# A two-layer decoder trunk: 32 of 80 modulation pieces scaled by ScalarE and added by GpSimd's transfers in place of VectorE

## The chip, the cores and the metric

The kernel runs on one core of a Trainium2 chip, as one launch. The metric is the device time of that launch in microseconds (us). An execution under the profiler gives the trace that is read below; its own time stands beside its span.

## The reference, cut to what matters

Two layers over 256 tokens of 1024 features, all in float32:

```python
mod = silu(c) @ w_ada + b_ada                  # 6 parts of 1024: sh1, sc1, gt1, sh2, sc2, gt2
h = rmsnorm(x, g_pre_mix) * (1 + sc1) + sh1
... = split(h @ w_in)                          # queries, keys, values, index heads, gates
x = x + gt1 * rmsnorm(mixed @ w_out, g_post_mix)
h = rmsnorm(x, g_pre_ffn) * (1 + sc2) + sh2
f = (silu(h @ w_gate) * (h @ w_up)) @ w_down   # 2816 hidden features
x = x + gt2 * rmsnorm(f, g_post_ffn)
```

`mixed` is the gated sum of two attentions. The modulation `mod` depends only on the vector `c`. It is a product of a row of 1024 with a matrix of 1024 x 6144 in each layer, so its work is mostly the reading of 24 MB of weights.

## The kernel before, in words

**Products.** Every matrix product of weights runs on TensorE as three passes: high part times high part, high times low, low times high. ScalarE makes the high part of a weight unit (`split_hi`, L769, a rounding copy of 128 x 2048), VectorE the low part (`split_lo`, L1156, unit minus high part). Units of 1 MB come from one stream in memory through three buffers (`raw`) and go on to a ring of five split units (`w_hi`, `w_lo`). SyncE, called SP here, issues their loads (L579); a load waits until VectorE has split the unit that had the buffer.

**The feed-forward part** works through 11 blocks of 256 hidden features. In block j TensorE makes gate and up products for token tile 0, then for tile 1 (`up`), then the down products of block j-1 for tile 0, turns the gated products of block j for both tiles (`turn_m`, L1853), and makes the down products for tile 1. For each tile ScalarE takes the silu (L906) and VectorE multiplies it with the up product (`gate_m`, L1224). ScalarE and VectorE then split the turned products into high and low parts (`m_hi_split`, L862; `m_lo_split`, L1458). ScalarE's order in a block is: split of the unit `ahead`, silu of tile 0, silu of tile 1, split of the first unit `behind`, high parts of both turned tiles, split of the second unit `behind`.

In layer 1, blocks 5, 6 and 8, 9 go in pairs as a twin (seven products in place of eight). Twins need sums of the input over token tiles and halves (`add_tokens`). These are made in two parts, between the two `gate_m` calls of a block: part 0 (L1195 to L1197) in the block before `sums_step`, part 1 (L1189, L1191) in block `sums_step`. For layer 1 `sums_step` is 2. For layer 0, which has no twins, it is 11, so that part 0 runs in block 10.

**Modulation.** The 10 tables that are not made at the start are each made of 8 pieces of `w_ada` (128 x 1024, 512 KB); pieces are counted from 0 to 79. SP loads a piece (L589) into one of two slots (`ada`, `ADA_RING` = 2), once the piece two before it has been used. VectorE multiplies it with a column of silu(c) and adds it to the table's buffer in one instruction (`add_pieces`, L1284) and so frees the slot. After 8 pieces GpSimd sums over the partitions (`reduce`, L666, two all-reduces), loads the table's gains over the buffer (`finish`, L673, a transfer that GpSimd issues) and VectorE combines the two (`make_table`, L1343); for a shift table GpSimd copies the sum instead (L677). There are three such buffers. Each is first zeroed and given its bias by GpSimd (`seed`, L656 and a transfer of 4 KB, L659).

Pieces 0 to 23 and 48 to 71 are used in the mixing parts, 24 to 47 in layer 0's feed-forward part, 72 to 79 in layer 1's. `ffn_pieces(l)` gives their number for each block, and the blocks in which `make_table` stands. Of three pieces in a block, one is used after the split of the unit `ahead`, one before and one after the second unit `behind`. The order of work on each engine is written out by hand; SP issues weight and piece loads from one queue, in the same order in which they are used. The table that is made last (layer 1's gt2) is needed by the closing norm.

Of the kernel before, what the change touches and what calls it, by code (L numbers as in the profile page):

```python
# [13 lines left out]
KT = D // P  # L14
# [182 lines left out]
def mix_pieces(l, s):  # L197

    return (MIX_PIECES | {1: (1, 0), 2: (2, 1)} if l else FIRST_PIECES).get(s, (0, 0))
TOP_STEPS = range(5, 5 + N_TOP // 16)  # L200


def ffn_pieces(l):

    if l + 1 < DEPTH:
        return (0, 2, 3, 3, 3, 3, 3, 3, 2, 2, 0), (4, 8)
    return (2, 2, 3, 0, 0, 0, 0, 0, 1, 0, 0), (10,)

# [42 lines left out]
def hybrid_decoder_trunk(nc, x_in, c_in, const_in, c_row, scale_first, shift_first, w_ada, b_ada, gains, w_stream, out):  # L251
    with ExitStack() as ctx:
# [147 lines left out]
        s_m = sem("m_ready")  # L400
        s_adause = sem("ada_used")
        s_table = sem("table_made")
        s_dve = sem("dve_chain")
# [57 lines left out]
        def piece_at(n):  # L461

            return ada[:, n % ADA_RING, :], s_ada[n % ADA_RING], 16 * (n // ADA_RING + 1)

        def mm_no(c, t):
# [79 lines left out]
        def sums_step(l):  # L545

            return TWINS[l][0] - 3 if TWINS[l] else N_FF

# [12 lines left out]
        def _(sp):  # L561
# [19 lines left out]
            def load_pieces(count):  # L581
                for _ in range(count):
                    n = pieces[0]
                    l, part = MADE[n // KT]
                    dst, landed, _ = piece_at(n)
                    if n >= ADA_RING:
                        sp.wait_ge(s_adause, n - ADA_RING + 1)
                    k = n % KT
                    sp.dma_start(dst, w_ada[l, k * P:(k + 1) * P, part * D:(part + 1) * D]).then_inc(landed, 16)  # L589
                    pieces[0] += 1  # L590
# [52 lines left out]
        def _(pool):  # L643
# [17 lines left out]
            def reduce(n, i):  # L661

                pool.wait_ge(s_adause, KT * (n + 1))
                for half in range(2):
                    cols = slice(512 * half, 512 * half + 512)
                    nc.gpsimd.partition_all_reduce(acc[:, cols], tables[i][:, cols], P,  # L666
                                                   bass.bass_isa.ReduceOp.add).then_inc(s_reduced, 1)
                    pool.wait_ge(s_reduced, 2 * n + half + 1)

            def finish(n, i, l, which):  # L670
# [47 lines left out]
            for l in range(DEPTH):  # L718
# [18 lines left out]
                if more:  # L737
                    pool.wait_ge(s_h, 8 * l + 4)
                    seed(scale_t, l + 1, SC1, s_bias[1])
                    seed(shift_t, l + 1, SH1, s_bias[2])  # L740
                finish(n + 3, 0, l, 3)
                if more:
                    pool.wait_ge(s_table, 4 * l + 3)
                    finish(n + 4, 1, l + 1, 0)
                    pool.wait_ge(s_table, 4 * l + 4)
                    finish_shift(n + 5, 2 * l + 2)
# [3 lines left out]
        def _(act):  # L750
            def split_hi(l, u, part=None):
# [17 lines left out]
                nc.scalar.activation(w_hi[:, U % RING, a:n], src[:, a:n], ACT.Copy).then_inc(s_hi, 1)  # L769

            def copy_chunk(l, c, t):
# [136 lines left out]
            def twin_hi(l, j):  # L908
# [16 lines left out]
                m_hi_split(l, j, 0)  # L925
                m_hi_split(l, j, 1)
                split_hi(l, behind[6])
                split_hi(l, behind[7])
                m_hi_split(l, j + 1, 0)
                m_hi_split(l, j + 1, 1)  # L930

            def sum_squares(n):
# [100 lines left out]
            for l in range(DEPTH):  # L1033
# [60 lines left out]
                call_root(2 * l)  # L1094
                border(l, True)
                for j, *both in ffn_steps(l):
                    if both:
                        twin_hi(l, j)
                        continue
                    ahead, behind = up_splits(l, j)  # L1100
                    for u in ahead[:1]:
                        split_hi(l, u)
                    if j == 1:
                        m_hi_split(l, 0, 1)
# [13 lines left out]
                    if j < N_FF - 1:  # L1118
                        split_hi(l, behind[0])
                        if j:  # L1120
                            m_hi_split(l, j, 0)
                            m_hi_split(l, j, 1)
                        split_hi(l, behind[1])
                    else:
                        split_hi(l, behind[1])
                        call_root(2 * l + 1)
                        m_hi_split(l, j, 1)
# [4 lines left out]
        def _(dve):  # L1132
# [50 lines left out]

            def add_tokens(l, part):

                upper, lower = slice(0, 4), slice(4, KT)
                one, two = slice(0, P), slice(P, 2 * P)
                if part:
                    link(nc.vector.scalar_tensor_tensor(out=sums[:, upper, one], in0=sums[:, lower, two], scalar=-1.0,  # L1189
                                                        in1=sums[:, upper, one], op0=ALU.mult, op1=ALU.subtract))  # L1190
                    nc.vector.scalar_tensor_tensor(out=sums[:, lower, one], in0=sums[:, lower, one], scalar=-1.0,  # L1191
                                                   in1=sums[:, upper, one], op0=ALU.mult, op1=ALU.subtract).then_inc(s_sums, 1)
                    return
# [3 lines left out]
                link(nc.vector.tensor_tensor(sums[:, upper, two], sums[:, upper, one], sums[:, upper, two], ALU.subtract))  # L1197

            def sums_low(l):
# [26 lines left out]
            def twin_lo(l, j):  # L1226
# [23 lines left out]
                many = ffn_pieces(l)[0][j]  # L1250
                add_pieces(max(many - 2, 0))
                split_lo(l, behind[6])
                add_pieces(min(many, 1))
                split_lo(l, behind[7])
                add_pieces(many > 1)
                m_lo_split(l, j + 1, 0)
                m_lo_split(l, j + 1, 1)

            def split_lo_half(l, u, half):
# [11 lines left out]
            def add_pieces(many):  # L1271

                for _ in range(many):
                    m = pieces[0]
                    k, part = m % KT, m // KT
                    buf = tables[part % 3]
# [4 lines left out]
                    dve.wait_ge(landed, count)  # L1281
                    if m:
                        dve.wait_ge(s_adause, m)
                    nc.vector.scalar_tensor_tensor(out=buf[:, :], in0=src, scalar=cs[:, k:k + 1],  # L1284
                                                   in1=buf[:, :], op0=ALU.mult, op1=ALU.add).then_inc(s_adause, 1)
                    pieces[0] += 1

# [350 lines left out]
            for l in range(DEPTH):  # L1638
# [54 lines left out]
                for j, *both in ffn_steps(l):  # L1693
# [10 lines left out]
                    for t in range(TT):  # L1704
# [659 lines left out]
```

## Time and profile before

| | |
|---|---|
| median of 3 runs | 850.3 us (849.49 to 850.66) |
| profiled execution, own time | 849.34 us |
| profiled execution, span | 847.6 us |
| TensorE, VectorE, ScalarE, GpSimd busy | 98%, 82%, 54%, 15% of the span |
| TensorE's mean granted clock | 0.997 |
| read from memory | 192.29 MB, 228 GB/s over the span |

A profile's times count from the start of its span. A busy TensorE need not be at its peak, because matmuls overlap: a 128 x 512 matmul lasts 0.39 us and the next one starts 0.23 us after it. Idle time of an engine that nobody waits for costs nothing. A wait is put down to the event that ended it.

### The profile page before, as it was taken

What the parts mean: (1) busy time and instruction counts of PE and PEld (TensorE: products, weight loads), DVE (VectorE), ACT (ScalarE), POOL (GpSimd) and SP (SyncE); (2) the same over time, 40 slices, a digit from 0 to 9 for tenths busy, and PEclk for the clock granted to TensorE, in tenths of its full rate; (3) what the DMA queues carried; (4) which work ended last, traced back from release to release, by engine and by line L of the source; (5) the groups of instructions that cost most, each with busy time, mean ns of one, the idle gap of its engine ahead of it and who ended that gap; (6) DMA issues with size and microseconds to landing.
All of it is one profiled execution on the core that took longest, in us unless ns stands there. A gap on an engine that the chain in (4) does not pass through costs nothing.

```text
span 847.6 us, 11588 instructions
## 1 busy us (share of the span) xinstructions
PE 833.1 (98%) x4131; PEld 690.4 (81%) x4131; DVE 693.0 (82%) x1183; ACT 458.7 (54%) x732; POOL 123.5 (15%) x92
## 2 busy tenths in 40 slices
PE   8999999999999999999999999999999989999997
PEld 6877888888888888888788788888888868888885
DVE  5898889888788777785889899898777886889974
ACT  5665555555666434433566556565565635554642
POOL 5500300302220021120420040040040000000021
PEclk9999999999999999999999999999999999999999
DMA  8996666575418888787338756766642586165341
GB/s 342 408 367 227 225 256 257 199 271 208 150 51 305 295 290 315 251 323 283 134 125 305 285 205 217 276 215 246 215 150 100 202 302 263 53 242 205 149 175 74
DMA packets 34795, 194.09 MB, mean 229 GB/s; under 512 B 4273, under 2 KB 4529, under 8 KB 17714
## 3 DMA queue, kind: packets, MB, share of 16 engines
q1 hardware_dynamic: 33410, 189.64, 60.6%
q0 software_dynamic: 1328, 3.71, 1.2%
q8 instruction: 33, 0.54, 0.2%
q14 instruction: 24, 0.20, 0.1%
HBM read 192.29 MB, written 1.05 MB: 228 GB/s over the span
## 4 chain that ended last, share of the span: by engine, by line
PE 91%; DMA 4%; DVE 3%; ACT 1%; issue 1%; SPq 0%; DVEq 0%; ACTq 0%
PE ps L1740 24%; PE ps L1742 23%; PE ps L1741 23%; PE ps L2159 5%; PE ps L1853 4%; DMA wide_t<-scale_first 3%; PE ps L1917 2%; PE ps L1777 1%; PE ps L1778 1%; PE ps L1784 1%; PE ps L1938 1%; PE ps L1939 1%; PE ps L1916 1%; PE ps L1937 1%; PE ps L1899 1%
## 5 line engine op out<-in xcount | busy, mean ns | idle before, releaser
L1156 DVE TENSOR_TENSOR w_lo<-raw,w_hi 128x2048 fp32r<-128x2048 f32 (+2 forms) x126 | 286.1, 2277 | 48.6 <-ACT w_hi L769 47.4
L1740 PE MATMUL ps<-w_hi,t_hi 128*128 128x512 f32 (+2 forms) x712 | 282.0, 396 | 1.1 <-DVE w_lo L1156 0.9
L1742 PE MATMUL ps<-w_hi,t_lo 128*128 128x512 f32 (+2 forms) x712 | 275.1, 386 | 0.0
L1741 PE MATMUL ps<-w_lo,t_hi 128*128 128x512 f32 (+2 forms) x712 | 274.5, 386 | 0.0
L769 ACT ACTIVATE w_hi<-raw 128x2048 fp32r<-128x2048 f32 (+2 forms) x128 | 240.5, 1883 | 34.8 <-DMA raw<-w_stream 26.0
L666 POOL PARTITION_ALL_REDUCE wide_t<-wide_t x20 | 82.0, 4098 | 591.0 <-DVE wide_t L1284 590.1
L1740 PEld LDWEIGHTS ps<-w_hi,t_hi 128*128 128x128 f32 x712 | 133.8, 188 | 29.7 <-DVE w_lo L1156 1.9
L1742 PEld LDWEIGHTS ps<-w_hi,t_lo 128*128 128x128 f32 x712 | 133.7, 188 | 27.7
L1741 PEld LDWEIGHTS ps<-w_lo,t_hi 128*128 128x128 f32 x712 | 134.0, 188 | 25.1
L1284 DVE SCALAR_TENSOR_TENSOR wide_t<-ada,cs,wide_t 128x1024 f32<-128x1024 f32 x80 | 110.3, 1378 | 0.4
L1740 PE MATMUL ps<-w_hi,m_hi 128*128 128x512 f32 x208 | 85.2, 410 | 0.0
L1742 PE MATMUL ps<-w_hi,m_lo 128*128 128x512 f32 x208 | 82.0, 394 | 0.0
L1741 PE MATMUL ps<-w_lo,m_hi 128*128 128x512 f32 x208 | 81.6, 392 | 0.0
L906 ACT ACTIVATE relu<-ps 128x256 f32<-128x256 f32 x38 | 14.5, 383 | 107.7 <-PE ps L1742 107.7
L842 ACT ACTIVATE qkT<-ps 128x512 f32<-128x512 f32 x24 | 14.4, 598 | 72.1 <-PE ps L1853 45.5
L1742 PEld LDWEIGHTS ps<-w_hi,m_lo 128*128 128x128 f32 x208 | 39.4, 189 | 8.8
L1740 PEld LDWEIGHTS ps<-w_hi,m_hi 128*128 128x128 f32 x208 | 39.4, 190 | 8.1 <-DVE m_lo L1458 0.9
L1741 PEld LDWEIGHTS ps<-w_lo,m_hi 128*128 128x128 f32 x208 | 39.6, 191 | 7.4
L1224 DVE TENSOR_TENSOR ffn_m<-relu,ps 128x256 f32<-128x256 f32 x38 | 15.7, 416 | 35.8 <-ACT relu L906 35.7
L796 ACT ACTIVATE pj<-ps 128x384 f32<-128x384 f32 x32 | 15.7, 491 | 38.6 <-PE ps L1742 38.6
L862 ACT ACTIVATE m_hi<-ps 128x256 fp32r<-128x256 f32 (+1 forms) x48 | 17.3, 398 | 18.3 <-PE ps L1853 18.3
L769 ACT ACTIVATE w_hi<-mixed 128x2048 fp32r<-128x2048 f32 x9 | 17.3, 1920 | 12.2 <-DVE mixed L1168 9.5
(257 smaller groups left out, 1080.4 us busy)
## 6 DMA issues: line engine op xcount, KB each, us to landing
raw<-w_stream SPq DMA_DIRECT2D x124, 1024.0 KB, 5.2
ada<-w_ada SPq DMA_DIRECT2D x80, 512.0 KB, 5.6
wide_t<-gains POOLq DMA_DIRECT2D x7, 512.0 KB, 4.7
mixed<-w_stream SPq DMA_DIRECT2D x3, 1024.0 KB, 8.5
raw<-w_stream SPq DMA_DIRECT2D x4, 656.0 KB, 7.1
mixed<-scale_first SPq DMA_DIRECT2D x2, 1024.0 KB, 10.4
wide_t<-shift_first SPq DMA_DIRECT2D x4, 512.0 KB, 11.1
wide_t<-scale_first SPq DMA_DIRECT2D x2, 1024.0 KB, 12.7
```

What stands on the lines that cost most here:

```text
L666: nc.gpsimd.partition_all_reduce(acc[:, cols], tables[i][:, cols], P, bass.bass_isa.ReduceOp.add).then_inc(s_reduced, 1)
L769: nc.scalar.activation(w_hi[:, U % RING, a:n], src[:, a:n], ACT.Copy).then_inc(s_hi, 1)
L796: nc.scalar.activation(dst[:, 0:384], src[:, 0:384], ACT.Copy)
L862: nc.scalar.activation(dst, src, ACT.Copy).then_inc(s_act_hi, 1)
L1156: nc.vector.tensor_tensor(w_lo[:, U % RING, a:n], src[:, a:n], w_hi[:, U % RING, a:n].bitcast(F32), ALU.subtract).then_inc(s_lo, 1)
L1284: nc.vector.scalar_tensor_tensor(out=buf[:, :], in0=src, scalar=cs[:, k:k + 1], in1=buf[:, :], op0=ALU.mult, op1=ALU.add).then_inc(s_adaus ...
L1740: nc.tensor.matmul(dst, hi, w_h, start=first, stop=False)
L1741: nc.tensor.matmul(dst, hi, w_l, start=False, stop=False)
L1742: return nc.tensor.matmul(dst, lo, w_h, start=False, stop=last)
L1853: ins = nc.tensor.transpose(dst[:, i * P:(i + 1) * P], blk, ident)
L1917: nc.tensor.matmul(ps[:, SCO, P:3 * P], q[:, P:SEQ], k, start=True, stop=True).then_inc(s_sco, 1)
L2159: ins = nc.tensor.matmul(ps[:, bank, :], h[:, k, tokens], w[:, U % RING, cols], start=first and i + n == 0, stop=i + n == 5, skip_group_ch ...
```

## The change

It does five things. Pieces 24 to 47 and 72 to 79 (`by_transfer`) are scaled in place by ScalarE, with the column of silu(c) as scale, and then added to the table's buffer by a transfer that GpSimd issues, memory to memory on the chip, with an addition in the transfer. Each adding transfer waits for the one before it to land (for a table's first piece, for its bias). The slot of such a piece is free, and a table complete, when the transfer has landed. In layer 1's feed-forward part the pieces are spread as 1, 1, 1, 1, 1, 0, 0, 1, 2, 0, 0 over the blocks, in place of 2, 2, 3, 0, 0, 0, 0, 0, 1, 0, 0. `add_tokens` runs whole in block `sums_step`, and in layer 0 not at all. In a twin block the pieces stand one before the last unit's split and the others after the turned products' split.

```diff
+def by_transfer(n):
+    return n // KT % PARTS >= 3
@@ ffn_pieces
-    return (2, 2, 3, 0, 0, 0, 0, 0, 1, 0, 0), (10,)
+    return (1, 1, 1, 1, 1, 0, 0, 1, 2, 0, 0), (10,)
@@
+        def pieces_before(n, transfers):
+            return sum(by_transfer(m) == transfers for m in range(n))
+
+        def wait_piece(eng, n):
+            if by_transfer(n):
+                eng.wait_ge(s_added, 16 * pieces_before(n + 1, True))
+            else:
+                eng.wait_ge(s_adause, pieces_before(n + 1, False))
@@ sums_step
-            return TWINS[l][0] - 3 if TWINS[l] else N_FF
+            return TWINS[l][0] - 3 if TWINS[l] else 2 * N_FF
@@ SP, load_pieces
                     if n >= ADA_RING:
-                        sp.wait_ge(s_adause, n - ADA_RING + 1)
+                        wait_piece(sp, n - ADA_RING)
@@ GpSimd
             def reduce(n, i):
-                pool.wait_ge(s_adause, KT * (n + 1))
+                wait_piece(pool, KT * n + KT - 1)
...
+            def add_scaled(n, i):
+                for m in range(KT * n, KT * (n + 1)):
+                    if not by_transfer(m):
+                        return
+                    if m == KT * n:
+                        pool.wait_ge(s_bias[i], 16 * (n // 3 + 1))
+                    else:
+                        wait_piece(pool, m - 1)
+                    pool.wait_ge(s_scaled, pieces_before(m + 1, True))
+                    pool.dma_start(tables[i][:, :], piece_at(m)[0], accum_op=ALU.add).then_inc(s_added, 16)
...
+                add_scaled(n + 3, 0)
                 finish(n + 3, 0, l, 3)
                 if more:
+                    add_scaled(n + 4, 1)
                     pool.wait_ge(s_table, 4 * l + 3)
                     finish(n + 4, 1, l + 1, 0)
+                    add_scaled(n + 5, 2)
                     pool.wait_ge(s_table, 4 * l + 4)
                     finish_shift(n + 5, 2 * l + 2)
@@ ScalarE
+            def scale_pieces(many):
+                for _ in range(many):
+                    m = pieces[0]
+                    pieces[0] += 1
+                    if by_transfer(m):
+                        src, landed, count = piece_at(m)
+                        act.wait_ge(landed, count)
+                        nc.scalar.activation(src, src, ACT.Copy, scale=cs[:, m % KT:m % KT + 1]).then_inc(s_scaled, 1)
@@ ScalarE, a block of the feed-forward part
                     for u in ahead[:1]:
                         split_hi(l, u)
+                    scale_pieces(max(many - 2, 0))
...
                             m_hi_split(l, j, 1)
+                        scale_pieces(min(many, 1))
                         split_hi(l, behind[1])
+                        scale_pieces(many > 1)
@@ VectorE, add_pieces
                     m = pieces[0]
+                    pieces[0] += 1
+                    if by_transfer(m):
+                        continue
@@ VectorE, between the two gate_m calls
                         if t == 0 and j == sums_step(l):
-                            add_tokens(l, 1)
-                        elif t == 0 and j == sums_step(l) - 1:
-                            add_tokens(l, 0)
+                            add_tokens(l)
```

## Rows read from the trace of the kernel before

**Rows 1.** The page's part 1: busy time, share of the span, instructions of each engine
```profile
PE 833.1 (98%) x4131; PEld 690.4 (81%) x4131; DVE 693.0 (82%) x1183; ACT 458.7 (54%) x732; POOL 123.5 (15%) x92
```
**Rows 2.** TensorE's waits: total us, times, longest us
```profile
PE ps L1853 <- DVE ffn_m L1224: 5.4, 2, 3.7
```
**Rows 3.** Timeline, VectorE, end of layer 0: start, duration, instruction
```profile
414.48 3.35 DVE L1195 TENSOR_TENSOR token_sums<-t_hi,t_lo 128x2048 f32<-128x2048 f32 x1
417.86 2.62 DVE L1196 TENSOR_TENSOR token_sums<-token_sums 128x512 f32<-128x512 f32 x1
420.51 0.69 DVE L1197 TENSOR_TENSOR token_sums<-token_sums 128x512 f32<-128x512 f32 x1
...
423.41 0.41 DVE L1224 TENSOR_TENSOR ffn_m<-relu,ps 128x256 f32<-128x256 f32 x1
```
**Rows 4.** Timeline, VectorE and TensorE, layer 1's feed-forward block 1
```profile
680.42 2.29 DVE L1195 TENSOR_TENSOR token_sums<-t_hi,t_lo 128x2048 f32<-128x2048 f32 x1
...
684.19 0.42 DVE L1224 TENSOR_TENSOR ffn_m<-relu,ps 128x256 f32<-128x256 f32 x1
...
684.67 0.44 PE L1853 MATMUL ps<-const,ffn_m 128*128 128x128 f32 x2 [3.67 <-DVE ffn_m L1224]
```
**Rows 5.** Windows: us, engines busy (instructions), granted clock, DMA share, GB/s
```profile
686.00:688.00 2.00, 2.00 (x6) 1.52 (x6) 2.00 (x3) 1.33 (x1) 0.00 (x0) 0.50 0.19 78
```
**Rows 6.** One tile's or line's instructions: ns least/median/most, first and last start
```profile
L1284 DVE SCALAR_TENSOR_TENSOR wide_t<-ada,cs,wide_t x80: 1272/1280/3266, 50.0 to 818.6; 128x1024 f32<-128x1024 f32 x80
...
L1009 ACT ACTIVATE pj<-x,rstd x1: 1148/1148/1148, 9.9 to 9.9; 128x1024 f32<-128x1024 f32 x1
```
**Rows 7.** Timeline, ScalarE, layer 0: turned products of block 1, silu of block 4
```profile
270.91 0.66 ACT L862 ACTIVATE m_hi<-ps 128x256 fp32r<-128x256 f32 x2 [0.75 <-PE ps L1853]
...
312.92 0.39 ACT L906 ACTIVATE relu<-ps 128x256 f32<-128x256 f32 x1 [3.04 <-PE ps L1742]
```
**Rows 8.** The chain of waits: TensorE's turns in layer 0, then the border's norm
```profile
321.05 0.44 PE ps L1853 x4
...
337.86 0.44 PE ps L1853 x4
...
354.65 0.44 PE ps L1853 x4
...
388.25 0.44 PE ps L1853 x4
...
430.67 0.56 DVE pj L1530
```
**Rows 9.** Windows, one block of layer 0 (PE, PEld, DVE, ACT, POOL)
```profile
371.60:388.40 16.80, 16.80 (x78) 13.92 (x77) 10.70 (x10) 7.07 (x7) 0.00 (x0) 1.00 0.91 365
```
**Rows 10.** Landing times: layer 0's piece loads, then all gains and all bias transfers
```profile
DMA to landing us min/median/max: 3.5/5.8/7.5
...
DMA to landing us min/median/max: 3.8/4.7/7.8
...
DMA to landing us min/median/max: 1.7/1.8/6.9
```
**Rows 11.** Timeline, GpSimd: the reduction of table 3 in layer 0
```profile
311.45 8.53 POOL L666 PARTITION_ALL_REDUCE wide_t<-wide_t  x2 [57.73 <-DVE wide_t L1284]
320.27 0.55 POOL L673 DMA_DIRECT2D wide_t<-gains  x1 [0.30 <-POOL wide_t L666]
```
**Rows 12.** DMA issues from 371 to 388 us: median us to landing
```profile
raw<-w_stream SPq DMA_DIRECT2D x3, 1024.0 KB, 6.9
```
**Rows 13.** Timeline, ScalarE and VectorE, the end of layer 1
```profile
819.16 0.63 ACT L862 ACTIVATE m_hi<-ps 128x256 fp32r<-128x256 f32 x2
...
834.44 1.22 DVE L1343 SCALAR_TENSOR_TENSOR wide_t<-wide_t 128x1024 f32<-128x1024 f32 x1
...
838.26 1.42 DVE L1565 SCALAR_TENSOR_TENSOR x<-pj,rstd,x 128x512 f32<-128x512 f32 x2
...
841.28 0.15 DVE L1500 TENSOR_SCALAR base<-ssq 128x1 f32<-128x1 f32 x1 [1.60 <-ACT pj L951]
```

More of the change, by code:

```diff
@@ L401, in hybrid_decoder_trunk @@
         s_adause = sem("ada_used")
+        s_scaled = sem("ada_scaled")
+        s_added = sem("ada_added_by_transfer")
         s_table = sem("table_made")
@@ L769, in split_hi @@
                 nc.scalar.activation(w_hi[:, U % RING, a:n], src[:, a:n], ACT.Copy).then_inc(s_hi, 1)
+            pieces = [sum(sum(mix_pieces(0, s)) for s in range(N_CHUNK + 1))]
+            def scale_pieces(many):
[6 more added lines that the diff above has]
+                        nc.scalar.activation(src, src, ACT.Copy, scale=cs[:, m % KT:m % KT + 1]).then_inc(s_scaled, 1)
             def copy_chunk(l, c, t):
@@ L926, in twin_hi @@
                 m_hi_split(l, j, 1)
+                many = ffn_pieces(l)[0][j]
                 split_hi(l, behind[6])
+                scale_pieces(min(many, 1))
                 split_hi(l, behind[7])
@@ L930, in twin_hi @@
                 m_hi_split(l, j + 1, 1)
+                scale_pieces(max(many - 1, 0))
             def sum_squares(n):
@@ L1095, in _ @@
                 border(l, True)
+                if l:
+                    pieces[0] += sum(sum(mix_pieces(l, s)) for s in range(N_CHUNK + 1))
                 for j, *both in ffn_steps(l):
@@ L1100, in _ @@
                     ahead, behind = up_splits(l, j)
+                    many = ffn_pieces(l)[0][j]
                     for u in ahead[:1]:
                         split_hi(l, u)
+                    scale_pieces(max(many - 2, 0))
                     if j == 1:
@@ L1122, in _ @@
                             m_hi_split(l, j, 1)
+                        scale_pieces(min(many, 1))
                         split_hi(l, behind[1])
+                        scale_pieces(many > 1)
                     else:
@@ L1182, in add_corner, with add_tokens @@
                 nc.vector.tensor_tensor(w_sum, w_sum, stored(*SOURCE[U + 2])[0], ALU.add).then_inc(s_w_sum, 1)
-            def add_tokens(l, part):
+            def add_tokens(l):
                 upper, lower = slice(0, 4), slice(4, KT)
                 one, two = slice(0, P), slice(P, 2 * P)
[L1188 to L1193, printed above, removed]
                 dve.wait_ge(s_act_lo, l * N_SPLIT + turn_no("h2", 3))
@@ L1197, in add_tokens @@
                 link(nc.vector.tensor_tensor(sums[:, upper, two], sums[:, upper, one], sums[:, upper, two], ALU.subtract))
+                link(nc.vector.scalar_tensor_tensor(out=sums[:, upper, one], in0=sums[:, lower, two], scalar=-1.0,
+                                                    in1=sums[:, upper, one], op0=ALU.mult, op1=ALU.subtract))
+                nc.vector.scalar_tensor_tensor(out=sums[:, lower, one], in0=sums[:, lower, one], scalar=-1.0,
+                                               in1=sums[:, upper, one], op0=ALU.mult, op1=ALU.subtract).then_inc(s_sums, 1)
             def sums_low(l):
@@ L1250, in twin_lo @@
                 many = ffn_pieces(l)[0][j]
-                add_pieces(max(many - 2, 0))
                 split_lo(l, behind[6])
@@ L1254, in twin_lo @@
                 split_lo(l, behind[7])
-                add_pieces(many > 1)
                 m_lo_split(l, j + 1, 0)
                 m_lo_split(l, j + 1, 1)
+                add_pieces(max(many - 1, 0))
             def split_lo_half(l, u, half):
@@ L1281, in add_pieces @@
                     dve.wait_ge(landed, count)
-                    if m:
-                        dve.wait_ge(s_adause, m)
+                    if k:
+                        dve.wait_ge(s_adause, pieces_before(m, False))
                     nc.vector.scalar_tensor_tensor(out=buf[:, :], in0=src, scalar=cs[:, k:k + 1],
                                                    in1=buf[:, :], op0=ALU.mult, op1=ALU.add).then_inc(s_adause, 1)
-                    pieces[0] += 1
             def first_rms():
```

## The prediction

> **What bounds the kernel now.** I read the page's part 1 first [rows 1]: TensorE is busy for 98% of the span, VectorE for 82%, ScalarE for 54%. So work taken off VectorE is worth nothing by itself; only TensorE's idle time can be won. The table of waits has two such times behind VectorE, 5.4 us together [rows 2]. The timelines place both. At the end of layer 0, between the two gated products of block 10, VectorE adds token sums although layer 0 has no twin blocks; under the all-reduce of GpSimd these take 3.35 and 2.62 us in place of 2.29 and 0.69, and the second product starts at 423.41 [rows 3]. TensorE idles the smaller part, 5.4 - 3.7 = about 1.8 us (rounding included). In layer 1 the same sums, behind modulation pieces, let TensorE idle 3.67 us [rows 4]. After that idle time its granted clock is 0.50 of full between 686 and 688 [rows 5], the level of 1.2 in place of 2.4 GHz; six matmuls fit where nine do, and over the slow stretch that makes about 7 matmuls of 0.21 us more each, 1.5 us. What can be won: 1.8 + 3.7 + 1.5 = 7.0 us.
>
> **The change, part by part.**
>
> *VectorE* loses 32 pieces of 1.28 us [rows 6], 41 us in all, but all of it lies beside TensorE's work except at the place above in layer 1. There the second product ends at 684.6; without the piece just before (1.28) and the sums (684.19 - 680.42 = 3.8) it ends at 679.5, and TensorE needs it at 684.67 - 3.67 = 681.0. The wait goes, and so does its clock loss: -5.2. The sums in layer 0's last block go: -1.8; late next there is the root's table load on ScalarE, which ends at about the same time as TensorE's down products and is not waited for.
>
> *Token sums whole in block 2 of layer 1*: 2.29 + 4 x 0.69 = 5.05 us [rows 3, 4] now stand between the two gated products. A block's first silu starts 8.1 us before TensorE needs both products (312.92 against 321.05, [rows 7, 8]). 0.8 + 5.2 + 0.4 = 6.4, so 1.7 us of cover are left: 0.
>
> *ScalarE* gets 32 scalings of 1024 columns. The nearest row takes 1.15 us for that shape [rows 6]; behind another one I take 1.0. It has 16.8 - 7.1 = 9.7 us free in each block [rows 9], so the work itself costs 0. But it is in order, and it now waits for each piece to land, with the silu of the next block behind it.
>
> *GpSimd, SP and the ring of two pieces* carry the decision. Before, a piece's slot came free when VectorE had used it, 1.3 us after its turn. Now piece n+2 is loaded only after piece n has landed, been scaled, and been added; the additions are in series; and an all-reduce stands between two tables. Three durations matter. L, load of a piece to its landing: 5.8 in layer 0's blocks [rows 10]. T, an adding transfer of 512 KB from issue to landing: no row has one. Its bounds are GpSimd's own transfers: 1.8 for 4 KB and 7.8 for the slowest of 512 KB. The nearest row is the gains transfer, the same engine, size and kind of queue, median 4.7 [rows 10]; I take 4.7, since what a destination read adds and what the shorter source path saves are both unknown. R, the all-reduce with the gains transfer's issue behind it: 8.5 + 0.3 + 0.55 = 9.35 [rows 11].
>
> In layer 0 there are three pieces a block from block 2 to 7, all taken by ScalarE within 6 us: B after the m split, C after the next weight split, A before the next silu. Two pieces can be under way, so one link (load, scale, add) of 5.8 + 1.0 + 4.7 = 11.5 must fit into two thirds of 16.8 = 11.2. It nearly does, with no slack. Worked forward by: load starts at added(n-2); scaled = landed + 1.0, not before its place on ScalarE; added = the later of scaled and added(n-1), + 4.7. Piece 24 is scaled at 272.5, behind the m split [rows 7]. That gives added times 277.2, 281.9, 288.7, 294.0, 300.2, 305.5, 311.7, 317.0 for 24 to 31. TensorE turns the products of blocks 4, 5, 6, 8 at 321.05, 337.86, 354.65, 388.25 [rows 8]; ScalarE may reach the first silu up to 1.25 us before (two silus and a product). Piece 32 is scaled at 318.5, limit 319.8: still in time.
>
> Then table 3 is reduced, and no piece is added until 317.0 + 9.35 = 326.35. Piece 32 is added at 331.05, 33 at 335.75. Piece 34 waits for 32: landed 336.85, scaled 337.85. Piece 35, before block 5's silu, waits for 33: scaled 342.55, limit 336.6. **TensorE stalls 5.95 us.** Block 6 misses by 1.5 in the same way (piece 38, scaled 360.85, limit 359.35). At the second reduction, behind piece 39 (added 370.25), piece 40 lands at 370.25 + 9.35 + 4.7 = 384.3, 42 is scaled at 391.1, 43 at 395.8, the next weight split ends 397.7, limit 394.45: 3.25 more. The weight loads stand behind the piece loads on SP: one issued at 389.4 lands 6.9 later [rows 12], 0.5 us after ScalarE would want it. Sum 11.2. The clock falls after the two long stalls as in rows 5; 1.5 us after the first is swallowed by block 6's miss, 1.5 after the last counts: 12.7. The last shift table has its last piece at 427 and is reduced by 437; VectorE needs it where the border's first norm starts, 430.7 [rows 8] - 1.8 + 10.7 = 439.6: no cost.
>
> *Layer 1* has one piece in each of blocks 0 to 4, one in 7, two in twin block 8. With 16.8 us for one link of 11.5 that costs nothing, and fewer loads at its start help the weights. *The tail*: piece 79 can be scaled only behind the last m split, at 819.16 + 0.63 + 1.05 = 820.8 [rows 13]. Add T of 3.8 (the least of rows 10, since the queue is empty there) to 4.7, reduce 8.5, issue gains after 0.3, land 3.8, make the table 1.22: 838.5 to 839.4, where it was 835.66 [rows 13]. VectorE then finishes tile 0 at 842.5 to 843.4 in place of 839.7, and tile 1, which it began at 841.28, begins 1.2 to 2.1 late, of which up to 0.5 is won back from waits: about +1.5.
>
> **Sum** against the profiled execution's own 849.34: -7.0 + 12.7 + 1.5 = +7.2, so 856.5. The median of the runs is 850.3, 0.1% above that execution; I leave the number as it is. About 0.2%, 1.7 us, is what a measurement of this kernel can tell from no change.
>
> **The rivals.** *The transfers are quick, and it gets faster.* From piece 30 to the limit of block 5 stand four T in a row, R and one L; there is no stall if 4T + L is at most 19.6: with L 5.8 T may be 3.5, with the least L of rows 10, 3.5, it may be 4.0. The least gains transfer took 3.8. Then -7.0 + 1.0 leaves 843.3; between 3.6 and 4.2 the time climbs to 850. For it: the source lies in SBUF, and waits on ScalarE thin out traffic. Against: the median of its rows is 4.7 and the longest 7.8. The Trainium skill, "DMA: Bandwidth & Descriptors", section Anatomy of one DMA, fits a GpSimd transfer as 2.0 us plus its bytes over 436 KB per us. That is an estimated 3.2 us here and would give this rival's 843.3; the gains rows disagree, and no row shows an adding one. Chance 0.33, with its near-neutral edge.
>
> *The DMA engines fill up.* Their share in these blocks is already 0.91 at 365 GB/s in one of these blocks [rows 9]. Three additions of 0.52 MB a block take at 365 GB/s 4.3 us of 16.8, a quarter, and twice that if the destination is read as well. Then T and L both grow. Each microsecond of T costs 1.5 us in each of six blocks: T = 6.2 gives 870, T = 7.8 gives 885. VectorE holding GpSimd up adds to it, as in rows 3 in the other direction. The Trainium skill, "SBUF — State Buffer", Who interferes with whom, names a VectorE instruction with two SBUF inputs as contending with a GpSimd one that reads SBUF; rows 3 agree (3.35 for 2.29), but whether the writing of descriptors suffers no row shows. Chance 0.20.
>
> *The change's slip stays hidden*: ScalarE's order has more play than I count, and only the tail and the gain are left, 844 to 848. Chance 0.05, on the faster side.
>
> **How the numbers follow.** My forecast, stalls at the reductions with T from 4.2 to 5.5, reaches from 850 to 864: chance 0.42. The range must reach to the quick case below, 843, and into the full-engine case above, 876 (T near 6.9), leaving out about 0.15. Faster by over 0.2%: most of 0.33 and 0.05, 0.35. Within: 0.07, where T is near 4.2. Slower: 0.58.
>
> **What would show it.** Right: GpSimd's adding transfers land 4.2 us or more after issue; ScalarE waits for the landing of pieces 34, 35, 42, 43; SP waits for GpSimd's additions; TensorE idles behind the products of block 5 (about 6 us) and block 8, with a clock at 0.5 after; no token sums in layer 0; no idle time at the start of layer 1; the last table ready after 838 less 7 plus the shift. Wrong: adding transfers under 3.7 us, or ScalarE never late for a silu; then the time is 843 to 848.

## The result, and the profile after

The changed kernel takes **945.48 us** (median of 4, 944.01 to 947.10) where the kernel before takes 849.89 (median of 4): ratio **1.1125**, 95% interval 1.1103 to 1.1147. The forecast was 856.5 with a range from 843 to 876. Its sign is right, its size is far off. The profiled execution took 944.01, its span 942.2.

The page's parts 1, 2, 3 and 4 of the changed kernel: busy time by engine; TensorE and its granted clock in 40 slices of 23.6 us; GpSimd's DMA queue with its packets, MB and share of the 16 DMA engines' span; the chain that ended last, by engine.
```profile
PE 849.8 (90%) x4131; PEld 701.8 (74%) x4131; DVE 647.6 (69%) x1148; ACT 492.7 (52%) x764; POOL 145.7 (15%) x124
...
PE   8999999999999654865498799999999999999997
...
PEclk9999999999999777877889899999999999999999
...
q0 software_dynamic: 5936, 20.49, 10.3%
...
PE 63%; DMA 28%; POOL 3%; DVE 2%; issue 2%; ACT 1%; SPq 0%; DVEq 0%; POOLq 0%; ACTq 0%
```
Against [rows 1] VectorE is 45 us less busy, as intended, and TensorE fell from 98% to 90%. All that is lost lies in one place: slices 14 to 23 (306 to 542 us), the feed-forward part of layer 0 and the border behind it. What ended last is no longer TensorE's own work throughout; for 28% of the span it is DMA transfers.

The table of waits (engine, line, released by: us in total, times, longest), with the wait that answers to [rows 2] on line 1907:
```profile
POOL wide_t L701 <- DMA wide_t<-ada: 198.1, 23, 10.7
...
ACT w_hi L805 <- DMA raw<-w_stream: 96.2, 38, 4.7
...
ACT ada L817 <- DMA ada<-w_ada: 76.4, 22, 11.7
PE ps L1907 <- DVE ffn_m L1279: 75.6, 9, 15.1
```
TensorE's wait for the gated products is 75.6 us where it was 5.4 [rows 2]. GpSimd waits 23 times for an adding transfer (L701) to land, ScalarE 22 times for a piece.

The chain of waits, from the first adding transfer to the table that the border needs (start, duration, what):
```profile
271.81 1.05 ACT ada L817
...
273.45 4.49 DMA wide_t<-ada
...
278.24 9.75 DMA wide_t<-ada
...
288.27 9.62 DMA wide_t<-ada
...
348.12 3.24 POOL wide_t L687
...
356.47 6.55 DMA wide_t<-ada
...
363.30 9.66 DMA wide_t<-ada
...
527.25 1.04 POOL wide_t L710
528.38 0.56 DVE pj L1586
...
553.32 1.09 PE ps L1907 x10
```
From 273.45 on the chain is the 24 transfers of layer 0 one behind the other, with 0.3 us between a landing and the next issue, and the reductions between the tables. No work of TensorE, VectorE or ScalarE is on it until 528. VectorE's border work starts at 528.38, where it started at 430.67 [rows 8]: 97.7 us late. The block of TensorE that starts at 553.32 is in the kernel before at 454.59, so layer 0 costs 98.7 us. From there to the end it is 388.9 us in place of 393.0, which is 4.1 less. The sum, +94.6, is the difference of the two spans (942.2 - 847.6).

Against the same block in the kernel e2 below, which has the change's sums and no transfers (452.77), layer 0 is 100.6 longer. The two waits of TensorE between 250 and 540 (74.7 behind the products, 6.7 behind the border's norm) are 81.4 of it. The other 19 are matmuls at the lower clock: the same 964 are busy for 221.8 us here and for 202.6 in e2 (windows up to the block behind the border, the changed kernel first, then e2).
```profile
250.00:553.32 303.32, 221.81 (x964) 182.17 (x963) 123.91 (x147) 126.48 (x150) 51.11 (x43) 0.85 0.75 212
```
```profile
250.00:452.77 202.77, 202.57 (x964) 169.28 (x965) 153.65 (x171) 100.50 (x126) 33.03 (x19) 1.00 0.70 255
```
More windows of the changed kernel (engines busy with their instructions, granted clock, DMA share, GB/s) show both waits and clock: a stretch that still runs at full clock, one after a wait, and the whole part.
```profile
278.20:288.20 10.00, 10.00 (x48) 8.28 (x47) 2.46 (x3) 2.65 (x4) 0.86 (x1) 1.00 0.83 210
...
308.10:318.10 10.00, 4.57 (x13) 3.75 (x14) 3.04 (x3) 3.57 (x5) 0.85 (x1) 0.53 0.84 211
...
250.00:540.00 290.00, 208.49 (x880) 169.87 (x879) 112.91 (x122) 116.96 (x139) 48.82 (x40) 0.85 0.76 213
```
TensorE idles nine microseconds before line 1907 at 313.53, and the granted clock over that window is 0.53, near the level of 1.2 in place of 2.4 GHz. In these stretches the DMA engines are 0.83 busy and move only 210 GB/s; before, it was 365 GB/s at 0.91 [rows 9].

**Why a transfer takes 9.7 us.** The transfers' row (least, median, longest time from issue to landing) answers to the gains row of [rows 10], whose median was 4.7:
```profile
DMA to landing us min/median/max: 4.4/9.7/11.3
```
Timelines of GpSimd and of SP's queue at the second transfer:
```profile
278.24 0.86 POOL L701 DMA_DIRECT2D wide_t<-ada  x1 [3.85 <-DMA wide_t<-ada]
```
```profile
277.96 0.33 SPq L610 DMA_DIRECT2D ada<-w_ada  x1
278.33 0.43 SPq L600 DMA_DIRECT2D raw<-w_stream  x1
```
The first transfer landed at 277.94. That landing frees a slot, and it does two things at once: it lets SP issue the next piece and the weight unit queued behind it (0.5 + 1 MB, at 277.96 and 278.33), and it lets GpSimd issue the next transfer, whose 0.86 us of issue begin at 278.24. So a transfer in the series is issued together with 1.57 MB of loads, all but the first of each table. At the 365 GB/s of [rows 9] those need 4.3 us by themselves. The first transfer, with no such loads beside it, took 4.49.

The packets that the DMA engines moved tell what the 9.7 us are made of. Queue q1 is SP's loads, q0 is GpSimd's transfers (packets, MB, share of 16 engines' time). The first view runs from the second transfer's issue at 278.24 to 283.50, the other from there to its landing:
```profile
q1 hardware_dynamic: 219, 1.14, 86.1%
```
```profile
q0 software_dynamic: 144, 0.52, 58.8%
q1 hardware_dynamic: 69, 0.43, 24.9%
```
For 5.3 us no packet of the transfer moves, while 1.14 of the 1.57 MB of loads do. Then its 144 packets pass in 4.1 us. The first transfer, alone, moved its first packet after 1.5 us and was through in 2.6 more. Over all 32 transfers the first packet moves 5.3 us after issue in the median. So most of what is added to the 4.49 us is waiting behind the loads.

**The kernel before had this case already.** The slowest gains transfer, the 7.8 us of [rows 10], is the one at 365.62 us. SP's queue and GpSimd at that time, then the transfer's row (KB, us to landing):
```profile
365.44 0.33 SPq L589 DMA_DIRECT2D ada<-w_ada  x1
365.81 0.43 SPq L579 DMA_DIRECT2D raw<-w_stream  x1
```
```profile
365.62 0.55 POOL L673 DMA_DIRECT2D wide_t<-gains  x1 [0.30 <-POOL wide_t L666]
```
```profile
wide_t<-gains POOLq DMA_DIRECT2D x1, 512.0 KB, 7.8
```
A piece and a unit go out within 0.2 us of it, just as in the changed kernel. The median of 4.7 is of gains transfers that mostly have no such neighbours.

ScalarE, in the same stretch, is not what holds the series up:
```profile
281.90 1.15 ACT L817 ACTIVATE ada<-ada,cs 128x1024 f32<-128x1024 f32 x1 [4.41 <-DMA ada<-w_ada]
...
291.89 1.15 ACT L817 ACTIVATE ada<-ada,cs 128x1024 f32<-128x1024 f32 x1 [2.07 <-DMA ada<-w_ada]
```
A piece is scaled by 283.0, 5 us before the series can take it at 288.27. The piece loads themselves land after 3.9 us here in the median (seven between 277 and 348), sooner than the 5.8 of [rows 10].

### The profile page after: what moved, and what is told of

It is laid out like the page before. It is cut to its first block, busy times and chain, and to the rows that moved or that the text cites. A ratio compares the mean times of both kernels' runs of the same rounds, so it can differ in the third digit from the quotient of the medians.

```text
span 942.2 us, 11616 instructions
## 1 busy us (share of the span) xinstructions
PE 849.8 (90%) x4131; PEld 701.8 (74%) x4131; DVE 647.6 (69%) x1148; ACT 492.7 (52%) x764; POOL 145.7 (15%) x124
## 3 DMA queue, kind: packets, MB, share of 16 engines
q0 software_dynamic: 5936, 20.49, 10.3%
## 4 chain that ended last, share of the span: by engine, by line
PE 63%; DMA 28%; POOL 3%; DVE 2%; issue 2%; ACT 1%; SPq 0%; DVEq 0%; POOLq 0%; ACTq 0%
DMA wide_t<-ada 25%; PE ps L1794 15%; PE ps L1796 15%; PE ps L1795 15%; PE ps L2213 4%; PE ps L1907 3%; POOL wide_t L687 3%; DMA wide_t<-scale_first 3%; PE ps L1971 1%; PE ps L1831 1%; PE ps L1832 1%; PE ps L1838 1%; PE ps L1993 1%; PE ps L1992 1%; PE ps L1970 1%
## 5 line engine op out<-in xcount | busy, mean ns | idle before, releaser
L687 POOL PARTITION_ALL_REDUCE wide_t<-wide_t x20 | 76.9, 3844 | 319.3 <-DVE wide_t L1341 287.9
L1794 PE MATMUL ps<-w_hi,m_hi 128*128 128x512 f32 x208 | 90.7, 436 | 0.3 <-DVE m_lo L1514 0.2
L1795 PE MATMUL ps<-w_lo,m_hi 128*128 128x512 f32 x208 | 86.5, 416 | 0.0
L1796 PE MATMUL ps<-w_hi,m_lo 128*128 128x512 f32 x208 | 86.1, 414 | 0.0
L1907 PE MATMUL ps<-const,ffn_m 128*128 128x128 f32 x88 | 17.6, 322 | 75.6 <-DVE ffn_m L1279 75.6
L701 POOL DMA_DIRECT2D wide_t<-ada x32 | 27.2, 851 | 356.5 <-DMA wide_t<-ada 198.1
L817 ACT ACTIVATE ada<-ada,cs 128x1024 f32<-128x1024 f32 x32 | 36.8, 1150 | 76.4 <-DMA ada<-w_ada 76.4
L1907 PEld LDWEIGHTS ps<-const,ffn_m 128*128 128x128 f32 x88 | 12.1, 159 | 81.9 <-DVE ffn_m L1279 79.2
L1341 DVE SCALAR_TENSOR_TENSOR wide_t<-ada,cs,wide_t 128x1024 f32<-128x1024 f32 x48 | 65.3, 1361 | 0.3
L1794 PEld LDWEIGHTS ps<-w_hi,m_hi 128*128 128x128 f32 x208 | 42.8, 206 | 9.2 <-DVE m_lo L1514 1.1
```

The lines of the kernel that those rows point to most:

```text
L701: pool.dma_start(tables[i][:, :], piece_at(m)[0], accum_op=ALU.add).then_inc(s_added, 16)
L817: nc.scalar.activation(src, src, ACT.Copy, scale=cs[:, m % KT:m % KT + 1]).then_inc(s_scaled, 1)
L1794: nc.tensor.matmul(dst, hi, w_h, start=first, stop=False)
L1795: nc.tensor.matmul(dst, hi, w_l, start=False, stop=False)
L1796: return nc.tensor.matmul(dst, lo, w_h, start=False, stop=last)
L1907: ins = nc.tensor.transpose(dst[:, i * P:(i + 1) * P], blk, ident)
```

## The experiments

Every kernel ran beside the kernel before, whose medians were 850.06 to 850.68. Line numbers shift by a few lines from kernel to kernel; the statement is the same.

### What of the change is not the transfers: e1, e2, e6

e1 is the kernel before with the sums whole in block 2 of layer 1 and none in layer 0:
```diff
-                            add_tokens(l, 1)
-                        elif t == 0 and j == sums_step(l) - 1:
-                            add_tokens(l, 0)
+                            add_tokens(l)
```


> The kernel before with the token sums alone changed: none in layer 0, whole in block 2 of layer 1; all 80 pieces stay with VectorE and keep their places. If the terms of the prediction hold (-1.8 at layer 0's last block, -3.7 and -1.5 at layer 1's block 1), it is 7 us faster than before: about 843. The rival, that layer 1's idle time came from late weight loads and the pieces rather than from the sums, gives -1.8 to -3 only (847 to 848).

Measured: 844.63, ratio 0.994 (0.9927 to 0.9953), 5.6 us less. The one wait for the products that is left stands in block 2 (TensorE's waits of e1):
```profile
PE ps L1849 <- DVE ffn_m L1222: 1.5, 1, 1.5
```
e2 is the changed kernel with all pieces on VectorE, spread as the change spreads them:
```diff
-    return n // KT % PARTS >= 3
+    return False
```


> The changed kernel with no piece given to the transfers: its token sums and its spread of layer 1's pieces over the blocks, everything scaled and added by VectorE. Theory: the transfers alone cost the 95 us, so this is 843 too, within 1 us of the sums alone. Rival: the spread or the new order in the twin blocks costs something of its own, which would show as 844 to 850.

Measured: 843.49, ratio 0.9925 (0.9913 to 0.9937), 6.7 less, with 0.6 us of that wait left. e6 keeps ScalarE's 32 scalings and drops the adding transfers:
```diff
-                eng.wait_ge(s_added, 16 * pieces_before(n + 1, True))
+                eng.wait_ge(s_scaled, pieces_before(n + 1, True))
...
-                    pool.dma_start(tables[i][:, :], piece_at(m)[0], accum_op=ALU.add).then_inc(s_added, 16)
```


> The changed kernel without the adding transfers: ScalarE scales the 32 pieces, a slot is free when its piece is scaled, and nothing is added, so these tables lack their products. Theory, the series of transfers sets the pace: without them TensorE waits for nothing in the blocks and the time is 842 to 845. Rival, ScalarE standing in order before piece landings is by itself a bound: 850 or more, with TensorE idle behind the silu products.

Measured: 843.49, ratio 0.9922 (0.9903 to 0.9941). What follows: moving the sums is worth 5.6 us, and 6.7 with the spread of layer 1's pieces (the intervals overlap, so the spread's own share isn't shown). Taking 41 us of work off VectorE is worth nothing beyond that, and scaling on ScalarE costs nothing. All of the loss is the transfers and the waits for them.

### Where the transfers cost: e3, e10, e11

e3 leaves transfers to the 8 pieces of the last table, in layer 1:
```diff
-    return n // KT % PARTS >= 3
+    return n >= 72
```


> Only pieces 72 to 79, in layer 1, go by transfer. Theory: with one piece in a block of 16.8 us a transfer of 10 us is hidden, and only the tail costs 1 to 1.5 us by the later last table: 844 to 845, 1 us slower than with all pieces on VectorE. Rival: the transfers disturb the weight loads wherever they stand; then TensorE waits in layer 1 and the time is over 848.

Measured: 844.01, ratio 0.9931 (0.9918 to 0.9945). Its transfers landed after 7.2 us in the median, and the wait for the products is 0.9 us, against 0.6 in e2: one piece in 16.8 us hides that. The time is what was expected. e10 adds table 3 of layer 0, and no other of layer 0:
```diff
-    return n // KT % PARTS >= 3
+    return 24 <= n < 32 or n >= 72
```


> Transfers for one table in layer 0 (pieces 24 to 31) and for layer 1's eight. Theory: the pace is 10 us a piece while they last: eight take 5 + 7 x 10 = 75 us, from 273.5 to 348, against block 3's end at about 310 with VectorE; the slack of 8 to 10 us comes off and the later pieces go back to VectorE at once: 25 to 30 us over the 844 of layer 1 alone, 868 to 875. Rival: the cost lies in the reductions between tables, or in all tables together; then one table costs under 12.

Measured: 876.08, ratio 1.0301 (1.0264 to 1.0339), against e3 32 us for eight transfers, just over the range given. It has no reduction between two series of transfers, and it still waits for the products (TensorE's waits of e10):
```profile
PE ps L1907 <- DVE ffn_m L1279: 27.0, 4, 10.6
```
e11 cuts the three reductions of layer 0's tables to 32 of 512 columns each half:
```diff
-                    cols = slice(512 * half, 512 * half + 512)
+                    cols = slice(512 * half, 512 * half + (512 if not (3 <= n < 6) else 32))
```


> The changed kernel with the all-reduces of layer 0's three transferred tables cut from 512 to 32 columns each (their sums over the partitions are left out for the rest). Theory: each reduction of 7.5 us stands in the series and is paid in full there, two between tables and one before layer 1; 942 falls by 15 to 22 us. The prediction had put nearly all of the loss here. Rival: reductions hide beside loads, and it falls by under 8.

Measured: 935.69, ratio 1.1002 (1.0962 to 1.1043). The reductions became 15.9 us shorter (7.48 to 1.16, 7.48 to 3.30, 6.55 to 1.16), the kernel only 9.8, between what the theory and the rival gave. The first transfer behind the first reduction takes 11.7 us here, where it took 6.55, and the one behind the second 8.3 in place of 6.39: a reduction gave the loads time to drain. So the place at which the forecast put the whole loss is worth some 10 of 95 us.

### Why a transfer lands so late: e4, e5, e7, e8

e4 lets the transfer copy instead of add; e5 moves a quarter of the bytes:
```diff
-                    pool.dma_start(tables[i][:, :], piece_at(m)[0], accum_op=ALU.add).then_inc(s_added, 16)
+                    pool.dma_start(tables[i][:, :], piece_at(m)[0]).then_inc(s_added, 16)
```
```diff
-                    pool.dma_start(tables[i][:, :], piece_at(m)[0], accum_op=ALU.add).then_inc(s_added, 16)
+                    pool.dma_start(tables[i][:, 0:256], piece_at(m)[0][:, 0:256], accum_op=ALU.add).then_inc(s_added, 16)
```


> The changed kernel with the 32 transfers copying instead of adding, so that a table holds its last piece only. Theory A, loads crowd the transfer out: alone 4.4 us, 9.7 with 1.5 MB of loads issued at the same moment; if the adding itself is cheap, copies land in 9 to 9.7 and the time stays above 930. Theory B, the adding is slow in the DMA engines: copies land in 5 to 6.5 as the gains transfers do, the series keeps up with the blocks or nearly, and the time is 850 to 870.

> The changed kernel with adding transfers of 256 of the 1024 columns (128 KB in place of 512), so that three quarters of each product are left out. If the time is in the bytes (A or B), the landing falls from 9.7 to 3.5 to 5 us and the kernel takes 843 to 850. If it is a fixed latency of an adding transfer behind loads, landing stays over 8 us and the time over 920.

Measured: e4 898.54, ratio 1.0567 (1.0522 to 1.0612), landing 7.8; e5 886.28, ratio 1.0423 (1.0389 to 1.0457). Neither gave what either theory expected. The rows of e5 (page part 6: KB of one, median us to landing) and of e4 (part 3):
```profile
wide_t<-ada POOLq DMA_DIRECT2D x32, 128.0 KB, 6.9
```
```profile
q0 software_dynamic: 5936, 20.49, 6.1%
```
A quarter of the bytes takes away 2.8 of 9.7 us. Some 6 us of the landing don't depend on the transfer's size: in e5 the first packet moves 4.6 us after issue in the median, and 1.2 MB of loads before it. And the same packets and bytes cost the DMA engines 10.3% of 942.2 us when they add and 6.1% of 895.7 when they copy; without about 11 us for the queue's other transfers (1.3% of 843.1 in e2), that is 2.7 against 1.4 us for each of the 32: adding takes the DMA engines twice as long. GpSimd's issue of one took 0.85 us to add and 0.53 to copy.

e7 leaves out the loads of the pieces concerned, so that no load follows a landing by way of the slots; e8 also copies:
```diff
                     n = pieces[0]
+                    if by_transfer(n):
+                        pieces[0] += 1
+                        continue
...
-                        act.wait_ge(landed, count)
+                        wait_piece(act, m - ADA_RING)
```


> The changed kernel without the loads of the 32 pieces: ScalarE scales what lies in the slot once the transfer two before has landed, and SP never waits for a transfer, so the tables hold wrong products. Theory A: with 1 MB units alone beside it, no longer issued at its landing, the adding transfer lands in 6 to 7.5 us; three need 19 to 23 us with GpSimd's own part, so the kernel takes 860 to 900. If the ring's load between two uses of a slot were the pace, it is 845. If an adding transfer has a fixed 9.7 us, the time stays over 925.

> Both at once: no loads of the 32 pieces and copies instead of additions (the products are left out). Theory: landing 4 to 5 us, close to the gains transfers, and the kernel at 842 to 848, as without any transfer. If it stays over 860, the series of waits itself, not the DMA engines, holds ScalarE up.

Measured: e7 894.44, ratio 1.0519 (1.0485 to 1.0552), as expected; e8 851.45, ratio 0.9999 (0.9978 to 1.002), seven of its eight runs between 847.59 and 854.17 and one of 865.58. It is slower than the 842 to 848 expected and under the 860 of the other reading. The landing times of all, worked together (median us; "first" is the first transfer of layer 0, which has no released loads beside it; "least" is the shortest of all 32):

| transfer | first | least | with the piece and unit loads | without the piece loads |
|---|---|---|---|---|
| adds, 512 KB | 4.5 | 4.4 | 9.7 | 6.8 |
| copies, 512 KB | 3.6 | 2.8 | 7.8 | 5.7 |
| adds, 128 KB | 2.9 | 2.5 | 6.9 | |

The 7.8 us of the copies is what the one gains transfer beside such loads took in the kernel before. e8 comes near the forecast's T, for which 850 to 864 were given up to 5.5; its transfers take 5.7. Its waits for the products:
```profile
PE ps L1910 <- DVE ffn_m L1282: 6.1, 3, 4.7
```
That is near the forecast, but it doesn't test its working forward: without the piece loads the link of load, scaling and transfer isn't there. It shows that a series with a landing of 5.7 us nearly keeps up with three pieces in a block.

### The ring or the series, and the order of issue: e9, e12

e9 gives layer 0's pieces four slots in place of two:
```diff
+        piece_slots = (ada[:, 0, :], ada[:, 1, :], mixed[:, 0, :], mixed[:, 1, :])
+        def slot(n):
+            return n % 4 if 24 <= n < 48 else n % 2
```


> The changed kernel with four slots in place of two for pieces 24 to 47 (the two more lie in the buffer of the mixed heads, free there); all else is the same. A load then waits for the transfer four pieces back. Theory: the series of transfers sets the pace, not the ring, and a landing still releases a piece and a unit at once until the ring has run ahead; with them no longer tied the landing falls towards the 6.8 us seen without the loads, at best 8: 24 of them and three reductions take 215 us where 178 are free, so 865 to 925. Rival: the two slots are the bound; then four bring it to 843 to 850.

Measured: 944.32, ratio 1.1104 (1.1068 to 1.114): no gain, neither the 865 to 925 of the theory nor the rival's 850. Landing 9.6 and 9.9. SP's queue and GpSimd in e9:
```profile
283.03 0.33 SPq L621 DMA_DIRECT2D ada<-w_ada  x1
283.40 0.43 SPq L607 DMA_DIRECT2D raw<-w_stream  x1
```
```profile
283.30 0.86 POOL L712 DMA_DIRECT2D wide_t<-ada  x1 [9.17 <-DMA wide_t<-ada]
```
With four slots a landing still releases the loads, only of a piece further on, and 0.3 us ahead of the next transfer. This run also says that the link of two slots is not the bound here: more slots would have loosened it. The series of transfers is.

e12 turns the order around: SP issues what a landing releases only after GpSimd has issued its next transfer.
```diff
                         wait_piece(sp, n - ADA_RING)
+                        if by_transfer(n - ADA_RING) and (n - 1) % KT:
+                            sp.wait_ge(s_issued, pieces_before(n, True))
...
+                    nc.gpsimd.memset(posf[:, 0:1], 0.0).then_inc(s_issued, 1)
+                    pool.wait_ge(s_issued, pieces_before(m + 1, True))
```


> The changed kernel, but SP issues the loads that a landing releases only after GpSimd has issued the next adding transfer (a small write of GpSimd tells it), 1 us later than now. All products stay whole. Theory: the transfer lands late because 1.5 MB of loads, issued 0.3 us before it, are ahead of it at the DMA engines; with the transfer's descriptors first it lands in 5 to 7 us, the series runs at 5.5 to 7.5 a piece and the kernel takes 855 to 900. Rival: the engines share their time between the two queues whatever came first, or the adding is slow beside any traffic; then the landing stays over 9 us and the time over 935.

Measured: 914.11, ratio 1.0757 (1.0701 to 1.0813), 31 us less than the changed kernel. Page part 6 of e12, then its timeline:
```profile
wide_t<-ada POOLq DMA_DIRECT2D x32, 512.0 KB, 5.5
```
```profile
285.17 1.15 ACT L822 ACTIVATE ada<-ada,cs 128x1024 f32<-128x1024 f32 x1 [8.03 <-DMA ada<-w_ada]
...
286.89 0.85 POOL L704 DMA_DIRECT2D wide_t<-ada  x1 [7.78 <-ACT ada L822]
...
287.92 0.33 SPq L613 DMA_DIRECT2D ada<-w_ada  x1
288.29 0.81 SPq L601 DMA_DIRECT2D raw<-w_stream  x1
```
One microsecond of order takes the landing from 9.7 to 5.5, with the same loads and bytes. The time came out above what was expected, and the bracket behind the POOL line says why: the transfer now waits for ScalarE, since each piece is loaded only after the transfer ahead is issued. The loop of load, scaling and issue is the new bound, at some 8.6 us a piece. Of the landing, then, the order of issue is shown to be the cause; the time is won back by a third only (31 of the 102 us between the changed kernel and e2), because three pieces of 8.6 us still don't fit into 16.8.

The packets say how the DMA engines share their time between the two queues. In e12 from the transfer's issue at 286.89 to 292 (first view), and in e4, where it copies, from 281 to 284 (second view):
```profile
q0 software_dynamic: 144, 0.52, 69.2%
q1 hardware_dynamic: 42, 0.15, 7.2%
```
```profile
q1 hardware_dynamic: 106, 0.85, 67.0%
q0 software_dynamic: 99, 0.39, 31.9%
```
In e12 the transfer is through before the loads have moved more than 0.15 MB. In e4 the two queues move packet for packet, 99 against 106. The Trainium skill, "DMA: Bandwidth & Descriptors", Queues, rings and completion order, has each DMA engine take turns between the queues that it has work for, packet by packet. The copies of e4 agree with that. The adding transfers don't: beside the same loads none of the second one's packets moves for 5.3 us, and a small one (e5) waits as well. Why adding differs from copying here no run shows.

A better order alone would probably not have been enough. In e12 the DMA engines are busy for 0.86 of the time from 286 to 346 us:
```profile
286.00:346.00 60.00, 44.40 (x184) 35.88 (x183) 20.59 (x20) 26.83 (x28) 13.73 (x17) 0.86 0.86 251
```
At 8.6 us a piece that is 7.4 us of all 16 engines for a piece, its unit and its addition, and a third of a block has 5.6. This is an estimate from busy shares, and no run tested it.

### The best version

e2 (843.49) and e3 (844.01) are faster than both kernels, by 0.7% against the kernel before. They can't be told apart: the new place of the sums pays, and transfers only where one piece in 16.8 us is due do no harm.

## Why the prediction was wrong in size

- **The gain, -7.0: right.** e1 gave -5.6, e2 -6.7. That 41 us off VectorE, and the scalings on ScalarE, are worth nothing by themselves: right (e6 as e2). The sums' 1.7 us of cover in block 2 held but for 0.6 us with spread pieces; in e1, where pieces stand beside them, 1.5 us showed.
- **T = 4.7 from the gains transfers: the step that failed first.** It measured 9.7. The first one, alone, took 4.49, so as a price of a transfer by itself the row was good. But here nearly every transfer is issued beside a slot's loads, because the same landing releases both. The row for that case was in [rows 10]: its slowest gains transfer, 7.8, was issued within 0.2 us of a piece and a unit, and the forecast took the median of rows issued under other conditions. Adding, which takes twice the DMA engines' time and here stood behind the loads, is the rest, from 7.8 to 9.7; no row could tell it. "SP waits for GpSimd's additions" was written down as what would be seen, but what SP issues at that instant was not followed to the transfer beside it.
- **"Each microsecond of T costs 1.5 us in each of six blocks": wrong slope.** It treats the link of two slots as the bound: half of L + 1.0 + T for each piece, so 1.5 us a block for each microsecond of T. The transfers in series need T + 0.3 for each piece, so 3 us a block. With the forecast's L of 5.8 the series is the longer one from T = 6.2 on, and with the 3.9 measured from 4.3 on. At 9.7 a block's three take 3 x 10.0 = 30 us where a block had 16.8, and e9 confirms that the link is not the bound. From e7 (T 6.8), e4 (7.8) and e8 (5.7) to the changed kernel TensorE's idle time behind products and norm grows by 15, 21 and 19 us for each microsecond of T; six blocks by 3 would be 18. These runs differ in their loads as well, so this is a rough agreement. Counted on with the forecast's slope, T = 9.7 would have given 885 + 1.9 x 9 = 902. So of the 87.5 us missed about 45 are T, and 42 the slope with the clock.
- **Loss placed at the two reductions, 5.95 + 1.5 + 3.25: wrong place.** e10 loses 32 us without one between its transfers, and e11 won under 10 by shortening all three. The reductions' 7.5 us are in the series, but the transfer behind each of the first two lands about 3 us sooner and gives part of that back.
- **Clock, 1.5 us after a long stall: right in kind**, but nine stalls and 19 us (221.8 less 202.6).
- **The shift table at the border, "no cost": wrong.** Its reduction ends the chain, and VectorE waits for it until 528.38. Again T, times 24.
- **Layer 1 hidden: right** (e3; and 4.1 us less in that part, where -5.2 and +1.5 were forecast, -3.7).
- **The rival "the DMA engines fill up": right in part.** Adding takes twice the engine time, as it feared, T grew, and it was priced too low by the same slope. But L did not grow, it fell from 5.8 to 3.9, and the engines' share was 0.83, not above the 0.91 of [rows 9]. Most of the growth of T is a burst issued ahead of each transfer. That the engines' time would bind with a better order is only estimated above.

## What to carry to other kernels

When a transfer in series ends, list everything that its landing releases: if loads on another queue go out at the same moment as the next transfer in the series, price the transfer with those loads ahead of it, not by itself. Then compare the series' period with the time that a block allows; once it is over, every microsecond counts as often as there are transfers in the block. And when a row gives a price, look at the conditions of its slowest instance before taking its median: here the slowest had the neighbours that the new transfer would have. Work taken from an engine that TensorE didn't wait for was worth nothing here (41 us of it), and the chain that took its place cost 102.

## What the runs showed of the hardware that was not expected

- A GpSimd transfer of 512 KB from SBUF to SBUF that adds lands 4.5 us after issue when alone and 9.7 when SP has issued 1.57 MB of loads within 0.3 us of it; issued 1 us ahead of the loads it lands in 5.5.
- Beside the same loads, an adding transfer's first packet moved after 5.3 us, when most of the loads were through. Copies moved packet for packet with the loads (99 against 106 in 3 us).
- Adding takes the DMA engines twice the time of copying the same packets (2.7 against 1.4 us each), and GpSimd's issue 0.85 against 0.53 us. The engines were 0.83 busy at 210 GB/s.
- A quarter of the bytes (128 KB) shortens the landing beside loads only from 9.7 to 6.9 us.
- A reduction on GpSimd gives something back: the transfer behind the first one takes 6.55 in place of 9.7, since the loads have landed meanwhile; with the reduction cut short it took 11.7.
